# Streamed state-space chunks with all fronts first, and cache copies placed among later weight loads

## The reference, cut to what matters

```python
def ssd_scan(x, dt, A, Bm, Cm, D, h0, chunk):
    ...
    acs = jnp.cumsum(dtc * A.reshape(G, HG), axis=2)
    seg = acs[:, :, :, None] - acs[:, :, None, :]
    decay = jnp.exp(jnp.where(causal[:, :, None, None], seg, -jnp.inf))
    cb = jnp.einsum('bcign,bcjgn->bcijg', Cc, Bc)
    y = jnp.einsum('bcijgh,bcjghp->bcighp', cb[..., None] * decay * dtc[:, :, None], xc)
    to_end = jnp.exp(acs[:, :, -1:] - acs) * dtc
    states = jnp.einsum('bclgn,bclghp->bcghpn', Bc, xc * to_end[..., None])
    chunk_decay = jnp.exp(acs[:, :, -1])
    ...   # hc * dec + st from chunk to chunk; h_in is the state before each
    y = y + jnp.einsum('bclgn,bcghpn->bclghp', Cc, h_in) * jnp.exp(acs)[..., None]
    y = y + xc * D

def gated_rmsnorm(y, z, g):
    u = y * jax.nn.silu(z)
    u = u * lax.rsqrt(jnp.mean(u * u, axis=-1, keepdims=True) + RMS_EPS)
    return u * g

out = jnp.concatenate([att_out, ssm_out], axis=-1) @ w_out
new_k_sample = concat(cache_k, k)[keep:]      # and the same for v
```

## Time and profile before

| | us |
|---|---|
| median of 3 runs | 2377.42 (2374.26 to 2382.67) |
| the profiled execution | 2373.41 |
| its span, first to last instruction | 2371.6 |
| TensorE busy in the span | 2115.3 |
| VectorE busy | 1569.7 |
| ScalarE busy | 745.9 |
| GpSimd busy | 803.7 |
| state-space stage, 580.18 to 732.57 | 152.39 |

### The profile page before, as it was taken

One profiled execution on the slowest core, in us unless ns is written; L12 is line 12 of the kernel. 1 busy time (PEld: TensorE's weight loads), 2 busy tenths in 40 slices (PEclk: granted clock), 3 DMA queues, 4 the chain that ended last, 5 costly groups with the idle time before them and its releaser, 6 DMA issues.

```text
span 2371.6 us, 34439 instructions
## 1 busy us (share of the span) xinstructions
PE 2115.3 (89%) x12253; PEld 1753.5 (74%) x12253; DVE 1569.7 (66%) x3260; ACT 745.9 (31%) x1111; POOL 803.7 (34%) x498
## 2 busy tenths in 40 slices
PE   7978998998678997999999989999888888898983
PEld 7978995555343347999999989999766666676762
DVE  1155215564443331169888979997888888898988
ACT  2122113443321002234444355554333232332321
POOL 2323320000110003346676621113544445565550
PEclk9999998999887998999999999999999999999996
DMA  9999987884996563225555578889999999999992
GB/s 351 348 357 347 350 326 292 328 353 180 324 323 230 176 240 99 71 95 171 173 171 171 170 243 293 295 287 366 388 394 394 394 394 380 395 395 394 392 393 76
DMA packets 200412, 682.81 MB, mean 288 GB/s; under 512 B 18432, under 2 KB 84352, under 8 KB 194304
## 3 DMA queue, kind: packets, MB, share of 16 engines
q1 hardware_dynamic: 151696, 508.36, 60.6%
q0 software_dynamic: 46080, 167.79, 18.5%
q10 hardware_dynamic: 2544, 5.48, 0.6%
HBM read 618.78 MB, written 196.32 MB: 344 GB/s over the span
## 4 chain that ended last, share of the span: by engine, by line
PE 35%; DMA 24%; issue 20%; DVE 14%; POOL 3%; ACT 3%; SPq 0%; ACTq 0%; DVEq 0%; POOLq 0%
DMA overlay<-peer_v 17%; PE bank L188 8%; PE bank L189 8%; PE bank L190 8%; DVE arena L1778 3%; DMA overlay<-peer_u 3%; DVE overlay L1955 3%; DMA overlay<-w_in 2%; PE bank L1765 2%; POOL overlay L341 2%; POOL overlay L1401 2%; DVE arena L1773 2%; PE bank L602 2%; PE bank L586 1%; PE bank L652 1%
## 5 line engine op out<-in xcount | busy, mean ns | idle before, releaser
L188 PE MATMUL bank<-overlay 128*128 128x384 f32 (+4 forms) x2856 | 989.0, 346 | 133.2 <-DVE overlay L1959 82.5
L189 PE MATMUL bank<-overlay 128*128 128x384 f32 (+4 forms) x2856 | 968.2, 339 | 0.0
L190 PE MATMUL bank<-overlay 128*128 128x384 f32 (+4 forms) x2856 | 966.4, 338 | 0.0
L188 PEld LDWEIGHTS bank<-overlay 128*128 128x128 f32 x2856 | 556.4, 195 | 199.3 <-issue 114.7
L190 PEld LDWEIGHTS bank<-overlay 128*128 128x128 f32 x2856 | 555.4, 194 | 33.5
L189 PEld LDWEIGHTS bank<-overlay 128*128 128x128 f32 x2856 | 556.9, 195 | 29.9
L1401 POOL TENSOR_TENSOR overlay<-overlay 128x1024 fp32r<-128x1024 f32 x98 | 262.6, 2682 | 207.2 <-ACT overlay L1393 207.1
L1610 POOL DMA_INDIRECT arena<-peer_rows,arena x160 | 182.6, 1141 | 366.3 <-DVE arena L1773 340.5
L1610 POOL DMA_INDIRECT arena<-peer_v,arena x160 | 228.7, 1429 | 172.0 <-DVE arena L1778 159.3
L1778 DVE SCALAR_TENSOR_TENSOR arena<-arena 128x1024 f32<-128x1024 f32 x160 | 203.9, 1275 | 0.4
L1773 DVE SCALAR_TENSOR_TENSOR arena<-arena 128x1024 f32<-128x1024 f32 x160 | 193.3, 1215 | 6.1 <-DMA arena<-peer_rows,arena 6.1
(11 more groups left out here) (221 smaller groups left out, 2028.8 us busy)
## 6 DMA issues: line engine op xcount, KB each, us to landing
overlay<-peer_u SPq DMA_DIRECT2D x128, 512.0 KB
overlay<-peer_v SPq DMA_DIRECT2D x128, 512.0 KB
o_ks<-cache_k SPq DMA_DIRECT2D x16, 4088.0 KB, 27.8
o_vsall<-cache_vall SPq DMA_DIRECT2D x16, 4088.0 KB, 40.1
arena<-cache_kT SPq DMA_DIRECT2D x32, 896.0 KB, 11.3
arena<-cache_v SPq DMA_DIRECT2D x56, 512.0 KB, 6.6
arena<-w_out SPq DMA_DIRECT2D x48, 512.0 KB, 4.8
act<-arena SPq DMA_DIRECT2D x128, 192.0 KB
```

Of the source, the lines that this page charges most:

```text
L188: pe.matmul(out, lhs[0], rhs[0], start=start, stop=False)
L189: pe.matmul(out, lhs[0], rhs[1], start=False, stop=False)
L190: return pe.matmul(out, lhs[1], rhs[0], start=False, stop=stop)
```

## The change

The ten copies that `sp_ssd` issued in one piece are split: five (of cache_k) stay, four (of cache_v) stand among the weights of `sp_out`, and one behind the first four weights of the query projection. The state-space stage is reordered. All five fronts run first, each into its own buffers (those of x lie where the values of the attention and the z halves are, so ScalarE first waits for their stores), alternating between two sets of four banks. Then the chunks run so that the decay sums and masks of the next chunk stand before the end of this one, and the gating of a chunk stands in the next: x·dt, x·w, y, the squares and the root have two buffers each. The state product stands at the head of a chunk, not at its end. `silu` writes over z. A weight can be loaded only once x or z in its place is done with, so the weights wait for `y_full` and `u` of the chunks.

```diff
@@ sp_ssd
             for x in range(11, 16):
                 copy_cache(sp, 0, x)
-            for x in range(5):
-                copy_cache(sp, 1, x)
             dve_ssd.wait(sp, QT - 1, "hn")
             store(sp, t["o_hp"], hT[:, QT % 2])
@@ pe_ssd_run
+            def front(i):
+                r, sfx, c0, b0 = rows(i), "" if i < QT else "_s", i * P, 4 * (i % 2)
+                if i == 1:
+                    pe.wait_ge(att_kept, H)
+                if i >= 2:
+                    act_ssd.wait(pe, i - 2, "cb_kept")
+                    dve_ssd.wait(pe, i - 2, "wdiff")
...
+            def intra(i, q):
+                r = rows(i)
+                if q == 0:
+                    if i:
+                        dve_ssd.wait(pe, i - 1, "y_add")
+                    else:
+                        act_ssd.wait(pe, QT - 1, "cb_kept")
+                        dve_ssd.wait(pe, QT - 1, "wdiff")
+                dve_ssd.wait(pe, i, f"M{q}")
...
+            for i in range(TILES):
+                front(i)
+            seg(0, 0)
+            seg(0, 1)
+            for i in range(QT):
+                state(i)
+                intra(i, 0)
+                seg(i, 2)
+                inter(i)
+                intra(i, 1)
+                seg(i, 3)
+                intra(i, 2)
+                seg(i + 1, 0)
+                intra(i, 3)
+                seg(i + 1, 1)
+                if i:
+                    dve_ssd.wait(pe, i, "t_inter")
                     pe_ssd.count_done(i, "out_turned", turn_out(pe, i - 1, 0))
...
@@ act_ssd_run
             act.wait_ge(d_out, D_DONE)
+            act.wait_ge(stored, 16 * SSD_STORES)
...
             for i in range(TILES):
+                front(i)
+            decay(0, 0)
+            decay(0, 1)
+            for i in range(QT):
+                decay(i, 2)
                 if i:
+                    squares(i - 1)
+                decay(i, 3)
+                silu_z(i)
+                if i:
+                    root(i - 1)
+                decay(i + 1, 0)
+                decay(i + 1, 1)
+                if i:
                     pe_ssd.wait(act, i, "out_turned")
                     keep_out(act, i, i - 1, "out_kept", 0)
@@ dve_ssd_run
+            for i in range(QT):
+                r = rows(i)
+                new_state(i)
+                if i:
+                    gated(i - 1)
+                masks(i, 2)
+                pe_ssd.wait(dve, i, "inter")
+                carried(i, 0)
+                masks(i, 3)
+                if i:
+                    normed(i - 1)
+                inputs(i + 1)
+                if i + 1 < QT:
+                    decayed(i + 1)
...
+                skip(i)
+                masks(i + 1, 0)
+                pe_ssd.wait(dve, i, "y3")
+                dve_ssd.wait(dve, i, "t_inter")
+                dve_ssd.count_done(i, "y_add", dve.tensor_tensor(by_head(yb[i % 2], r), by_head(yb[i % 2], r), two_banks(6, r), ALU.add))
+                masks(i + 1, 1)
@@ sp_out
-            for v in range(8):
-                weights(v)
-            pe_ssd.wait(sp, QT, "cb")
+            for i in range(3):
+                dve_ssd.wait(sp, i, "y_full")
+                weights(2 * i)
+                dve_ssd.wait(sp, i, "u")
+                weights(2 * i + 1)
+                if i < 2:
+                    copy_cache(sp, 1, i)
+            pe_ssd.wait(sp, QT - 1, "inter")
+            dve_ssd.wait(sp, QT - 1, "hd")
+            weights(7)
+            pe_ssd.wait(sp, QT - 1, "state")
             pool_ssd.wait(sp, QT, "cmask1")
             sp.dma_start(lng, t["ln1_g"]).then_inc(ln_in, 16)
             sp.dma_start(lnb, t["ln1_b"]).then_inc(ln_in, 16)
+            dve_ssd.wait(sp, QT - 1, "y_full")
+            weights(6)
             residual(0)
             residual(1)
             for c in range(16):
                 weights(c + 8)
+                if c in (3, 9):
+                    copy_cache(sp, 1, 2 + c // 9)
                 b = c - 2 + 2
                 if 2 <= b < NB:
@@ sp_query
             for s in range(4):
                 sp.dma_start(uraw[s], t["peer_wq"][s]).then_inc(u_in[s], 16)
+            copy_cache(sp, 1, 4)
```

More of the change, by code:

```diff
@@ L821, in layer, with __init__ @@
         class Events:
[L824 to L830, removed]
+            def __init__(self, sem, order):
+                self.sem, self.seen = sem, 0
+                self.counts = {event: n + 1 for n, event in enumerate(order)}
             def count_done(self, i, name, instruction):
@@ L841, in layer @@
         seqs = range(NB)
[L842 to L852, removed]
+        def order(*parts):
+            return [(i, name) for i, names in parts for name in names.split()]
@@ new lines, in chunks, with fronts, by_seq @@
+        def chunks(*parts):
+            return [event for i in range(QT) for event in order(*((i + ahead, names) for ahead, least, names in parts if i + ahead >= least))]
+        def fronts(names):
+            return order(*((i, names) for i in range(TILES)))
+        def by_seq(*names):
+            return " ".join(f"{name}{b}" for b in seqs for name in names)
+        pe_ssd = Events(sem("pe_ssd"), fronts("x_turned sums") + order((0, "seg0 seg1")) +
+            chunks((0, 0, "state y0 seg2 inter y1 seg3 y2"), (1, 0, "seg0"), (0, 0, "y3"), (1, 0, "seg1"), (0, 1, "out_turned")) +
+            order((QT, "y0 seg2 y1 seg3 y2 y3 out_turned " + by_seq("state") + " last_turned")))
@@ new lines, in layer @@
+        act_ssd = Events(sem("act_ssd"), fronts("x_kept b_kept cb_kept eacs etot wexp") + order((0, "E0 E1")) +
+            chunks((0, 0, "E2"), (-1, 0, "sq0 sq1"), (0, 0, "E3 zsilu"), (-1, 0, "root"), (1, 0, "E0 E1"), (0, 1, "out_kept")) +
+            order((QT, "E2"), (QT - 1, "sq0 sq1"), (QT, "E3 zsilu"), (QT - 1, "root"), (QT, "out_kept sq0 sq1 root last_kept")))
+        dve_ssd = Events(sem("dve_ssd"), order((0, "wdiff"), (1, "wdiff"), (0, "xdt xw"), (2, "wdiff"), (3, "wdiff"), (4, "wdiff"), (0, "hd M0 M1")) +
+            [event for i in range(QT) for event in order(
+                (i, "hn"), (i - 1, "y_full u" if i else ""), (i, "M2 t_inter M3"), (i - 1, "var rstd n0 n1" if i else ""),
+                (i + 1, "xdt xw" + (" hd" if i + 1 < QT else " bmask")), (i, "xD"), (i + 1, "M0"), (i, "y_add"), (i + 1, "M1"))] +
+            order((QT - 1, "y_full u"), (QT, "M2 M3"), (QT - 1, "var rstd n0 n1"),
+                  (QT, "xD y_add " + by_seq("hd", "hn") + " t_inter y_full u var rstd n0 n1")))
@@ L853, in layer @@
+        pool_ssd = Events(sem("pool_ssd"), order((0, "X0 X1"), (QT, "dam cmask0 cmask1"), (0, "X2 X3")) +
+            order(*((i, "X0 X1 X2 X3") for i in range(1, TILES))))
+        SSD_STORES = 5 + 2 * NB
         normg_in = sem("normg_in")
@@ L1070, in dve_ssd_run @@
+            for b in seqs:
+                act_store_states(act, b)
+            squares(QT)
+            root(QT)
+            pe_ssd.wait(act, QT, "last_turned")
+            keep_out(act, QT, QT, "last_kept", 4)
         def dve_ssd_run(dve):
```

394 lines of the change are left out of this document (209 added, 185 removed).

## The result

The changed kernel took 2352.61 us (median of four runs, 2348.01 to 2355.74) against 2378.19 for the kernel before beside it: a ratio of 0.9894, interval 0.9873 to 0.9916, or 25.6 us less. The profiled execution took 2350.70 with a span of 2348.9. Forecast were 2341 and a range of 2325 to 2358, so the time lies inside the range and 11.6 above the forecast.

The account below looks back on a forecast made before the run. Bound by a chain: each chunk's front, score, state and gating in sequence, no engine full. Stage -42.3, state-load stop +5.8, slow clock +2.1 gave -34.4 us, so 2341 (own range 2331 to 2350; 8 in 10, 2325 to 2358).

Parts of the forecast that it names:

- rival 2: State-space stage: VectorE meets GpSimd (POOL) products more than once per cycle, +10 us, 2351; chance 0.14 shared with late weights.
- fronts and first sums: Stage start to y0 of chunk 0: five fronts, two decay sums and the state product, 19.4 us (15.0 to 26).
- chunk 0: First chunk, from its y0 to the next: nothing to gate, 17.8 us, with 0.7 for meeting POOL.
- chunk 3 and sample tile: Last chunk 22.2 us, then 6.1 from the sample tile's y0 to the first out-projection product: 28.3.
- stop at the state load: Out-projection: h0[3] lands at 732.6, needed at 726.8, so TensorE stops 5.8 us (0 to 13).
- slow products behind it: Out-projection after the state-load stop: sixteen product rows at half clock take 9.18 against 7, +2.1 us.
- all behind: After the first out-projection pass: copies behind c = 9 and at the query cost 0 each, at most 13.0.
- One full cycle: Chunks 1 and 2, y0 to y0: ScalarE's chain to the root 13.1, then VectorE 9.2, 22.3 us each.
- rival 4: TensorE stays at its lower clock through the whole stage: stage 172 us, total 2397; chance 0.03.
- The DMA queue: SP's queue from o_hp to h0[3]: 3 copies 39.1, 21 pieces 26.9, latency 2.3, together 68.3 us.
- (1): Out-projection: state loads come in time, no stop, 2333; chance 0.15.
- Rival 3: Out-projection: the weights themselves come late, w4 after 717, up to 10 us, 2351; chance 0.14 shared with rival 2.

Follow-up runs that it names:

- Experiment 6: Late copies, with ScalarE's silu and its table load moved to the head of the chunk: 2339.91 us, ratio 0.9806 to the kernel before.
- Experiment 5: Late copies, with unused products filling TensorE's waits in chunks 2 and 3 and ahead of the sample tile: 2339.39 us, ratio 0.982 to the kernel before.
- the repeat: The changed kernel run again unaltered, beside two others on one chip, five rounds: 2348.07 us, ratio 0.9876 to the kernel before.
- late copies: The changed kernel with its third and fourth cache_v copies behind the weights of c = 9 and 12: 2341.07 us, again 2342.78.
- Experiment 7: Late copies, with VectorE waiting for ssm_norm_g only ahead of the first norm: 2341.44 us, ratio 0.9844 to the kernel before.
- experiment 1: The kernel before, old chunk order, with only its cache copies placed as in the change: 2390.98 us, ratio 1.0057 to the kernel before.
- experiment 4: The changed kernel with the first two cache_v copies issued ahead, behind the five of cache_k: 2348.23 us, ratio 0.9877 to the kernel before.
- experiment 2: The changed kernel with all ten copies issued ahead, as before: 2368.16 us, ratio 0.9956 to the kernel before.
- experiment 8: Late copies plus early silu, late wait for ssm_norm_g and six unused products before the sample tile's y0: 2327.66 us, ratio 0.9777.

## Why the prediction came out as it did

The mechanism was right in the main: a shorter stage, and one stop at the fourth state load. Most costs were taken too small, so that 25.3 us were gained of 34.4. The 2352.6 lies above the forecast's own range of 2331 to 2350. The wider range holds it only because rival 2 had stretched it upwards, and of that rival only 0.8 us came; that it holds is partly luck. (The change again, 2348.07, lies inside both.) In us, from the first transpose (0.1 of the sum is rounding):

| term | forecast | measured |
|---|---|---|
| fronts and first sums | 19.4 | 20.8 |
| chunk 0 | 17.8 | 18.7 |
| chunk 1 | 22.3 | 22.3 |
| chunk 2 | 22.3 | 24.0 |
| chunk 3 and sample tile | 28.3 | 30.1 |
| stage against before | -42.3 | -36.6 |
| stop at the state load | +5.8 | +3.7 |
| slow products behind it | +2.1 | +6.0 |
| slower start of the out-projection | 0 | +0.8 |
| all behind | 0 | +0.7 |
| sum | -34.4 | -25.3 |

**One full cycle.** The chain was the named one: E3, load, silu, load, root at 4.5, the reciprocal 0.03 behind the root, and behind it one product beside GpSimd (`xw`). Chunk 1 took 22.26, at a full clock: 13.4 to the root (forecast 13.1) and 8.8 from there (9.2), two small errors that offset each other. Experiment 6 confirms the chain from the other side.

**Chunks 2 and 3: the term that was mis-sized.** The sum took 22.3 for each, from rows at full clock, and did not ask what the cycle's own stops would do to the clock. Here two stops of 1.61 and 1.96 stand within 6 us. After them TensorE runs at its lower level for some 3.5 us, which costs 1.7 in chunk 2 and 1.7 in chunk 3. Experiment 5 filled the stops, and the 1.7 of chunk 3, which all seven traces without fills have, was gone. The 1.7 of chunk 2 is of another kind: three of the seven have it, and the profiled execution happened to be one; in the repeat chunk 2 took the forecast's 22.3. The prediction had the lower level as rival 4 only, as a state of the whole stage; it came in small pieces.

**Fronts.** 1.4 too cheap (0.7 to 1.9 in the six traces that still wait for ssm_norm_g and have no fills or early silu). VectorE's first instruction waits 8.87 for ssm_norm_g and starts 6.1 after the first transpose, where the forecast took the 4.6 of the earlier trace rows. That is the 1.4 and more: the start of VectorE hangs on a transfer, not on TensorE, and moves against it from one execution to the next (4.6 in the trace before, 5.5 and 6.6 in the repeats of late copies and of the change). Experiment 7 shows the wait to be worth 3.2 in all. It stands at the head of a whole engine for an operand that is first used 47 us later (the norm at 635.91).

**Chunk 0.** Of VectorE's products behind M3, two meet GpSimd, not one. The first meeting (L1187, 2.06) is in the sum; the second is the small product just ahead of y_add (L1258), which the sum took at 0.7:

```profile
619.53 1.52 DVE L1177 TENSOR_TENSOR arena<-arena 128x512 f32<-128x512 f32 x1
```

At 619.39 GpSimd begins its own, 1.12 long. That is 0.8 of the 0.9; it is read from the trace, and no experiment took it apart.

**The DMA queue.** o_hp to the landing of h0[3]: forecast 68.3, measured 69.4, and 68.0 in experiment 1. The stop is smaller (3.7) because the out-projection began later in relation to o_hp (28.4 behind it instead of 26.0) and itself started 0.8 slower, which offset the 1.1 of the queue and more: 5.8 + 1.1 - 2.4 - 0.8 = 3.7. Two things in the reasoning fell. The price of the stop's after-effect: states at 1.92 and 2.07 for 1.04 and 1.12 (7.7 in place of 4.1 for four pairs), then 6.11 for 3.70, together +6.0 where 2.1 was taken. And the picture of a backlog: in the change itself the DMA share was down to 0.86 from 715 to 721, just ahead of the third copy, and experiment 4 shows that with a half idle queue the copy ahead of the load costs nearly the same stop.

The rivals: the state loads were not in time (1), VectorE met GpSimd more often than taken only in chunk 0 (2), the weights were not late (3), no cycle held a drain (ScalarE's root starts 0.02 after its load), the clock held over most of the stage at 0.91 (4). Rival 3's mechanism is real where the copies stay ahead: 26.66 in experiment 2.

**Behind the first pass.** The copy at the query was taken at 0. TensorE's first wait for GpSimd's split there (`L188`) is 6.44 in place of 5.65, about the 0.7. It is 5.86 to 6.44 in all eleven traces with a copy there and 5.65 in the two without (before, experiment 2). ScalarE's three DMA issues just ahead of it take 2.69 in place of 1.90. No experiment moved this copy alone, so the link is read from the traces.

Left open: why the pair of stops ahead of chunk 2 brought the clock down in some executions only, and what makes the stretch ahead of the stage vary by up to 15 us (574 to 590) between executions of the same program.

## What to carry to other kernels

When a stage gets shorter, ask what its length was hiding: here it hid 130 us of copies, and each half of the change was worth far less, or less than nothing, without the other. Place a bulk copy where no small load that an engine waits for stands right behind it in the queue, or its whole length (here 13 us) is added to that load. When an overlap is summed up from rows, list TensorE's own short stops too and give the products behind them a range, from the full to the lower clock; a few unused products in such a wait can be cheaper than the wait (1.7 us in chunk 3 here). And before one trace's excess is given a cause, look at a second trace of the same kernel: of the two chunks that ran 1.7 long here, one did not in the repeat.

## What was not expected of the hardware

Short stops can bring the clock down, and not every time. One stop of 1.22 (622.24) did nothing, and chunk 1 ran at a granted clock of 1.00; nor did one of 2.61 among the fronts (589.41, the transposes behind it at 1.06). Stops of 1.61 and 1.96 with 2 us of products between them were followed by products at 1.91 for 1.02 in chunk 3 of the same trace and, in some form, in chunk 3 of all seven, but in chunk 2 in three of seven. In experiment 6 slow products followed a stop of 2.48, in experiment 8 they did not:

```profile
647.34 1.74 PE L1013 MATMUL bank<-arena 128*128 128x64 f32 x8 [2.48 <-DVE arena L1258]
```

```profile
631.50 1.10 PE L1013 MATMUL bank<-arena 128*128 128x64 f32 x8 [2.48 <-DVE arena L1265]
```

With the stops filled to 0.30 none were slow (one trace). The reverse took longer than the forecast: after 3.66 idle, the eight rows for the states and the eight of the out-projection took 13.7 (739.56 to 753.30) in place of 7.7, so TensorE was at the lower level for about 12 us of them. Behind the stops of 3.39, 4.98 and 8.00 in experiment 4, the repeat and experiment 1 they took 13.8, 12.6 and 12.9.

VectorE is slower beside GpSimd, and at times GpSimd too. A 128x1024 VectorE product takes 1.22 alone and 1.87 to 2.06 beside a GpSimd product. GpSimd's own takes 1.04 with VectorE idle (634.72), and 1.04 as well beside the 1.99 of the earlier trace rows (586.29); beside VectorE it is up to 2.12 in experiment 6 (642.35), and up to 1.48 in this trace:

```profile
615.92 1.48 POOL L919 TENSOR_TENSOR arena<-arena 128x512 f32<-128x512 f32 x1 [2.43 <-PE bank L999]
```

Moving VectorE by 2 us changed how many of its products were met. The Trainium skill (GPSIMD Engine Reference, Specifications) says that GpSimd's SBUF interfaces are shared with VectorE, with contention where the VectorE instruction has two SBUF inputs. The trace agrees: the slowed products all have two, and these are their numbers.

A load behind a copy in the same queue waits for all of it, even when the DMA engines had been half idle: 14.7 for 3.7 (experiment 4).
